# Moving the normalised activations by 32 bytes in SBUF, in a hybrid encoder block on one core

## What is computed

```python
h = rmsnorm(x, mix_norm_w);  u = h @ w_in
y_fox = fox_attention(q, k, v, f_logit, ...)      # 16 heads, 256 tokens
y_ssd = ssd_mixer(xs, Bm, Cm, z, dt_raw, ...)     # 16 heads, chunked scan
x = x + concat(y_fox, y_ssd) @ w_out
h = rmsnorm(x, ffn_norm_w)
g, up = split(h @ w_gate_up, [5632])              # 2048 x 11264
x = x + (silu(causal_dwconv(g)) * up) @ w_down    # 5632 x 2048
h = rmsnorm(x, ple_norm_w)
x = x + sigmoid(h @ w_ple_gate) * (p @ w_ple_proj)
out = rmsnorm(x, final_norm_w)
```

## The kernel before

| tensor | before | mod 64 | mod 128 | after | mod 64 | mod 128 |
|---|---|---|---|---|---|---|
| xtok | 16512 | 0 | 0 | 16512 | 0 | 0 |
| h_parts | 32896 | 0 | 0 | 32928 | 32 | 32 |
| w_raw | 65664 | 0 | 0 | 65728 | 0 | 64 |
| w_hi | 82048 | 0 | 0 | 82112 | 0 | 64 |
| w_lo | 98432 | 0 | 0 | 98496 | 0 | 64 |
| ident | 114816 | 0 | 0 | 114880 | 0 | 64 |
| pHi, pLo | 117440, 119488 | 0 | 64 | 117504, 119552 | 0 | 0 |
| rms | 121536 | 0 | 64 | 121600 | 0 | 0 |
| sumsq, sq | 124768, 126816 | 32 | 96, 96 | 124800, 126848 | 0 | 0, 0 |
| arena: qT, mixHi, act_parts | 128896 | 0 | 0 | 128896 | 0 | 0 |
| arena: conv_out | 211872 | 32 | 32 | 211872 | 32 | 32 |
| arena: ssd_row | 222112 | 32 | 32 | 222112 | 32 | 32 |

## Time and profile before

### The profile page before, as it was taken

One profiled execution on the slowest core, in us unless ns is written; L12 is line 12 of the kernel. 1 busy time (PEld: TensorE's weight loads), 2 busy tenths in 40 slices (PEclk: granted clock), 3 DMA queues, 4 the chain that ended last, 5 costly groups with the idle time before them and its releaser, 6 DMA issues.

```text
span 1260.5 us, 19756 instructions
## 1 busy us (share of the span) xinstructions
PE 1248.1 (99%) x7132; PEld 1081.4 (86%) x7132; DVE 821.5 (65%) x1107; ACT 622.0 (49%) x834; POOL 23.2 (2%) x34
## 2 busy tenths in 40 slices
PE   8999999999999999999999999999999999999997
PEld 7999998789888888888888888888888888888885
DVE  5698777678665676776767767676664454545554
ACT  6434565566545454444445444454444343445555
POOL 2000000001200000000000000000000000000000
PEclk9999999999999999999999999999999999999999
DMA  8566545334656566666666666656665656666662
GB/s 267 157 185 184 167 141 161 105 113 135 199 185 185 183 185 185 183 191 188 185 183 183 185 187 187 188 181 187 184 197 187 194 184 197 187 193 219 196 200 101
DMA packets 165884, 226.94 MB, mean 180 GB/s; under 512 B 10208, under 2 KB 101380, under 8 KB 165700
## 3 DMA queue, kind: packets, MB, share of 16 engines
q1 hardware_dynamic: 165732, 225.90, 58.9%
q0 software_dynamic: 96, 0.26, 0.1%
HBM read 224.03 MB, written 2.10 MB: 179 GB/s over the span
## 4 chain that ended last, share of the span: by engine, by line
PE 98%; DMA 1%; SPq 0%; ACT 0%; issue 0%; DVE 0%; ACTq 0%; DVEq 0%
PE ps L345 26%; PE ps L347 13%; PE ps L916 6%; PE ps L915 6%; PE ps L917 6%; PE ps L382 6%; PE ps L384 6%; PE ps L383 6%; PE ps L333 5%; PE ps L335 5%; PE ps L334 5%; PE ps L763 1%; DMA w_raw<-in_w_in 1%; PE ps L718 1%; PE ps L766 1%; PE ps L807 1%
## 5 line engine op out<-in xcount | busy, mean ns | idle before, releaser
L318 DVE TENSOR_TENSOR w_lo<-w_raw,w_hi 128x1024 fp32r<-128x1024 f32 x413 | 506.3, 1228 | 351.3 <-ACT w_hi L313 349.8
L313 ACT ACTIVATE w_hi<-w_raw 128x1024 fp32r<-128x1024 f32 x413 | 436.6, 1060 | 465.1 <-PE ps L347 233.4
L345 PE MATMUL ps<-h_parts,w_hi 128*128 128x512 f32 x1408 | 497.6, 399 | 0.0
L347 PE MATMUL ps<-h_parts,w_lo 128*128 128x256 f32 x1408 | 395.4, 281 | 0.0
L345 PEld LDWEIGHTS ps<-h_parts,w_hi 128*128 128x128 f32 x1408 | 264.5, 188 | 65.9
L347 PEld LDWEIGHTS ps<-h_parts,w_lo 128*128 128x128 f32 x1408 | 266.0, 189 | 0.0
L333 PE MATMUL ps<-h_parts,w_hi 128*128 128x256 f32 x576 | 165.9, 288 | 0.3 <-DVE w_lo L318 0.3
L335 PE MATMUL ps<-h_parts,w_lo 128*128 128x256 f32 x576 | 162.9, 283 | 0.0
L334 PE MATMUL ps<-h_parts,w_hi 128*128 128x256 f32 x576 | 162.8, 283 | 0.0
L915 PE MATMUL ps<-w_hi,act_parts 128*128 128x512 f32 x352 | 137.2, 390 | 0.0
L917 PE MATMUL ps<-w_hi,act_parts 128*128 128x512 f32 x352 | 137.0, 389 | 0.0
(11 more groups left out here) (238 smaller groups left out, 1081.0 us busy)
## 6 DMA issues: line engine op xcount, KB each, us to landing
w_raw<-in_w_gate_up SPq DMA_DIRECT2D x352, 256.0 KB, 3.1
w_raw<-in_w_in SPq DMA_DIRECT2D x88, 512.0 KB, 3.6
w_raw<-in_w_down SPq DMA_DIRECT2D x88, 512.0 KB, 4.4
w_raw<-in_w_out SPq DMA_DIRECT2D x32, 512.0 KB, 4.6
w_raw<-in_w_ple_gate SPq DMA_DIRECT2D x32, 512.0 KB, 4.5
w_raw<-in_w_ple_proj SPq DMA_DIRECT2D x4, 512.0 KB, 5.0
out_x<-xtok SPq DMA_DIRECT2D x8, 256.0 KB, 2.9
xtok<-in_x SPq DMA_DIRECT2D x3, 512.0 KB, 8.5
```

Source lines behind the costliest of these rows:

```text
L313: act.activation(parts(n)[0], w_raw[:, n % RING, :], ACT.Copy).then_inc(w_hi_made, 1)
L318: dve.tensor_tensor(lo, w_raw[:, n % RING, :], hi, ALU.subtract).then_inc(w_lo_made, 1)
L345: pe.matmul(ps[:, bank_of[m], :], hi, both.rearrange("p b t -> p (b t)"), start=first and k == 0, stop=False, skip_group_check=True)
L347: mm = pe.matmul(ps[:, bank_of[m], T:2 * T], lo, both[:, 0, :], start=False, stop=last and k == 1, skip_group_check=True)
```

## The change

Two small tensors are allocated at other places in the list. `eps` (4 bytes used, 32 taken) now stands between `xtok` and `h_parts`; `rms_col` (8 bytes used, 32 taken) stands between `h_parts` and `w_raw`. Nothing else in the program differs: the same instructions in the same order on every queue, the same sizes, the same waits.

```diff
         xtok = sb("xtok", [P, TT, D])
+        eps = sb("eps", [P, 1])
         h_parts = sb("h_parts", [P, KD, 2, T], F32R)
+        rms_col = sb("rms_col", [P, TT])
         hHi, hLo = h_parts[:, :, 0, :], h_parts[:, :, 1, :]
...
         rms = sb("rms", [P, 2, T])
-        rms_col = sb("rms_col", [P, TT])
         x_ssq = sb("x_ssq", [P, 2, TT, NDN])
...
         sq = sb("sq", [P, 2, T])
-        eps = sb("eps", [P, 1])
         arena = (nc.sbuf_base + 63) // 64 * 64
```

## The result

The changed kernel takes 1266.88 us (median of 7 runs, 1266.20 to 1268.91) against 1262.43 us for the kernel before (1262.13 to 1265.09): the ratio is 1.0033, with a 95% interval of 1.0021 to 1.0044. It is slower by a third of a percent, where I had forecast 1242 us.

A forecast was written before the change was run, and what follows sets the result against it. TensorE's unbroken matmul stream was taken as the bound, so start distances set the time: 1262.3 - 18.8 (FFN) - 11.5 (w_in) + 9.6 (w_down and w_out) = 1241.6, say 1242 us. Range 1228 to 1293 us.

The forecast's parts named there:

- What bounds the kernel: TensorE's unbroken matmul stream, busy 99% of 1260.5 us; addresses matter only through distances between matmul starts.
- the four distances that I said to look at: Start distances of FFN pairs (353.3 ns before), w_in (120.0), w_down (226.7) and w_ple_proj (233.3), to be checked afterwards.
- Step (a): h against the weights in w_in and the FFN: one 6.67 ns step less per streaming matmul, 30.3 us gained.
- Step (b): w_down and w_out, weights against arena operands: 1,440 matmuls gain a 6.67 ns step of distance, costing 9.6 us.
- pHi's extra step: In w_ple_proj, matmuls with pHi stationary stand 233.3 ns apart instead of 226.7, read as an address effect.
- Step (c): The 576 matmuls with h stationary: taken as 0, between -3.8 and +3.8 us.
- The vector and scalar side: VectorE and ScalarE work on moved h, sumsq and sq: costed at nothing, hidden under TensorE, cover thinnest in w_in.
- no effect: Rival: the excess belongs to float32r itself, not to addresses; 1262.5 us; no effect or a draw, chance 0.18.
- slower by the h streams: Rival: the 32-byte offset costs streaming matmuls of w_in and FFN one step more, 30.3 us, time 1293; chance 0.17.
- slower by the weights' 64 bytes alone: Rival: h streams gain nothing while w_down and w_out pay 9.6 us, time 1272; chance 0.16.
- My break-even: Saving per matmul streaming h at which the change breaks even: 9.6 us over 4,544 matmuls, 2.1 ns.
- the gain towards the floor: Remaining case: w_in and FFN distances fall towards their lowest possible, up to 66 us gained; chance 0.02.

The follow-up runs named there:

- a second interruption: The changed kernel with the two small `spread_rms` matmuls ahead of the FFN's sixth chunk issued twice: 1266.64 us, ratio 1.0034.
- TensorE alone: Programs computing none of the layer, only matmul streams at chosen address offsets with other engines idle; 226.7 ns between 512-column starts at offset 0.
- all three kernels that have them: Against the kernel before: h moved 32 and weights 128 bytes, 1261.21 us; small tensors regrouped around h, 1252.29 us (offset 224) and 1254.00 us (offset 96).
- the last experiment: Against the kernel before, only `eps` moved behind `rms_col`, shifting sumsq and sq by 32 bytes, matmul operands kept: 1262.47 us, ratio 1.0004.

## Why the prediction was wrong

**What bounds the kernel** was right: the time is the sum of distances between matmul starts, and their changes account for the 3.9 us. But the four distances that I said to look at were not enough: the one with h stationary, 2.9 us of the loss, was not among them.

**Step (a) failed.** I took a gain of one step for every matmul that streams h, 18.8 us in the FFN and 11.5 us in w_in, "because the FFN pair, where h streams, carries more than the plain excess and has been seen to lose a step without any change". At the offset that the change makes, 32, the pair has the rate of 353.3 ns in the kernel, with a second interruption, and with TensorE alone: the gain in the FFN was 0 (-0.2 us with the first chunks). In w_in it was 1.7 ns per matmul when steady, 2.9 us, and 2.2 us as summed, instead of 11.5. The faster rate of before said that a better state exists, not that this offset reaches it. Offsets 96 and 224 do reach it, in all three kernels that have them. Nor do the distances change in whole steps of 6.7 ns, by which I priced all parts: TensorE alone shows 228.3, 228.9, 231.9 and 234.5 ns for 512 columns.

**Step (b) had the right sign and three times the right size.** I priced w_out and w_down by pHi's extra step, 6.67 ns, on the ground that the weights would stand in "the relation in which pHi stood". They don't: pHi's address less the weights' is 64 by 256, act_parts' is -64, that is 192. I had worked by 128, in which the two are the same. At 192 the price is 2.0 ns in w_down and 2 in w_out: +3.0 us instead of 9.6.

**Step (c)** was costed at nothing, without a row for its offset, with 3.8 us as its bound. It came out near the bound: +2.9 us as summed. h as a stationary operand is mostly at offset 224, 233.3 ns. That is as much as w_out and w_down together.

**The vector and scalar side** at nothing was right, and the last experiment shows it. The rival "no effect" falls as a mechanism; with nothing else running the distance of float32r matmuls depends on the addresses. The Trainium skill, "SBUF — State Buffer", section "Who interferes with whom", says that TensorE never waits on anyone: the runs agree as far as the other engines go, since TensorE alone has the same 226.7 ns, but its two read ports don't make the place of its two operands indifferent. The rival "slower by the h streams" falls: the pairs stayed at 353.3 ns and w_in became faster. The rival "slower by the weights' 64 bytes alone" had the right effect at the wrong size and without (c); its forecast of 1272 us was 5 over. My break-even, 2.1 ns per streaming matmul, was reckoned with the wrong price of (b); with the measured 3.0 + 2.9 us it is 1.3 ns, and the streams gained 0.5 on average. The recorded chances also don't quite match their parts: the forecast and the gain towards the floor make 0.49 for faster, not 0.48, and the two slow rivals 0.33, not 0.34.

What stays open: what in TensorE or SBUF makes float32r matmuls depend on the offset, since neither the number of stationary columns nor the other engines explain it; and what chooses between the two rates of a pair at offsets 0 and 16, and of 256 columns at 64.

## What to carry to other kernels

Where TensorE streams float32r without a gap, measure the distance between matmul starts and compare it with the columns by the clock; then price a new layout per operand pair by stationary address less moving address, by 256, not by how round an address is. Moving one tensor shifts every relation in which it or anything allocated behind it takes part: 64 bytes of padding that seemed neutral cost w_down and w_out 3 us. A short program that runs the same stream at several offsets gave the time of the whole kernel to within 2 us at offsets 96 and 224, but was 7 us off at 16, where a stream has two rates. It gives steady distances, and a stage with interruptions can gain less: w_in at offset 96 gained 2.4 us instead of 4.7.

## What the runs showed that I had not expected

Float32r matmuls of 512 columns behind one another take 226.7 ns at offset 0 and 228.3 to 234.6 ns at the fifteen other multiples of 16 bytes below 256; those of 256 columns take 113.3 to 120.1 ns, with offset 0 among the slowest. The best offset for one form is the worst for another. Bfloat16 streams, 216 ns, showed no such thing at the two offsets tried. And the same pairs at offset 0 ran at 346.7 ns in one stretch and at 353.3 in the next: in the kernel before 24 of them at the faster rate and then, behind an interruption, the rest of the loop at the slower one, over 400 us without a return. No run here shows the faster rate at offset 0 for longer than 30 pairs.
